# A fused transformer block on one core: where the bias corner is masked, where the DRAM weight sums are issued, and the order of folds and splits in the FFN

## What is computed

```python
def first_block(x, ...):
    h = rms_norm(x, g_pre_mix)
    x = x + rms_norm(chunk_relpos_attention(h, w_qkv, w_o, rel_bias), g_post_mix)
    h = rms_norm(x, g_pre_ffn)
    x = x + rms_norm((silu(h @ w_gate) * (h @ w_up)) @ w_down, g_post_ffn)
    return x
# attention: 16 heads of 64; chunk c of 64 tokens sees the chunks max(0, c-8)..c;
# scores get rel_bias[head, clip(512 + i - j, -63, 128) + 63], then softmax, then @ v
```

## Time and profile before

| | us |
|---|---|
| median of 3 runs | 1453.14 |
| lowest, highest | 1451.38, 1453.32 |
| the profiled execution | 1452.84 |
| its span | 1451.1 |
| PE busy in it | 1293.3 (89%) |
| DVE busy | 806.8 (56%) |
| ACT busy | 624.9 (43%) |
| POOL busy | 83.3 (6%) |

### The profile page before, as it was taken

One profiled execution on the slowest core, in us unless ns is written; L12 is line 12 of the kernel. 1 busy time (PEld: TensorE's weight loads), 2 busy tenths in 40 slices (PEclk: granted clock), 3 DMA queues, 4 the chain that ended last, 5 costly groups with the idle time before them and its releaser, 6 DMA issues.

```text
span 1451.1 us, 18423 instructions
## 1 busy us (share of the span) xinstructions
PE 1293.3 (89%) x7031; PEld 1106.7 (76%) x7031; DVE 806.8 (56%) x1469; ACT 624.9 (43%) x1169; POOL 83.3 (6%) x145
## 2 busy tenths in 40 slices
PE   9998354545998898889999999999999999999998
PEld 7886242433897898888877888888887878898987
DVE  5374222332675554458776656777554553687574
ACT  5374222332544343345554543246433553354543
POOL 1011111111100000000001101000000000000000
PEclk9999676767999999999999999999999999999999
DMA  6479999999743544444653449941222213244542
GB/s 220 138 205 322 269 291 268 272 267 284 205 145 127 193 146 145 151 169 177 213 190 117 146 142 309 308 125 58 87 89 87 87 37 109 88 150 155 174 144 89
DMA packets 41448, 250.32 MB, mean 173 GB/s; under 512 B 5000, under 2 KB 5260, under 8 KB 13840
## 3 DMA queue, kind: packets, MB, share of 16 engines
q1 hardware_dynamic: 26952, 160.07, 31.1%
q0 software_dynamic: 11520, 83.89, 21.9%
q10 hardware_dynamic: 2888, 5.18, 1.0%
HBM read 240.72 MB, written 88.09 MB: 227 GB/s over the span
## 4 chain that ended last, share of the span: by engine, by line
PE 73%; DMA 18%; issue 3%; DVE 3%; ACT 1%; POOL 1%; ACTq 0%; SPq 0%; DVEq 0%; POOLq 0%
PE bank L2158 19%; PE bank L2160 19%; PE bank L2159 19%; DMA sum_dram<-in_weights 10%; DMA sum_dram<-sum_dram 8%; PE sc L2158 2%; PE sc L2160 2%; PE sc L2159 2%; PE sc L2335 1%; PE ob L2359 1%; PE tp L2344 1%; DVE w_lo L1349 1%; PE bank L2276 1%; POOL rstd L652 1%; PE bank L2285 1%
## 5 line engine op out<-in xcount | busy, mean ns | idle before, releaser
L1349 DVE TENSOR_TENSOR w_lo<-w_raw,w_hi 128x512 fp32r<-128x512 f32 (+1 forms) x427 | 331.4, 821 | 217.1 <-ACT w_hi L761 216.3
L2158 PE MATMUL bank<-xT_hi,w_hi 128*128 128x512 f32 (+1 forms) x960 | 360.5, 376 | 22.7 <-issue 22.6
L761 ACT ACTIVATE w_hi<-w_raw 128x512 fp32r<-128x512 f32 (+1 forms) x427 | 287.3, 728 | 172.5 <-PE bank L2160 124.8
L2159 PE MATMUL bank<-xT_lo,w_hi 128*128 128x512 f32 (+1 forms) x960 | 346.6, 361 | 0.0
L2160 PE MATMUL bank<-xT_hi,w_lo 128*128 128x512 f32 (+1 forms) x960 | 346.3, 361 | 0.0
L2158 PEld LDWEIGHTS bank<-xT_hi,w_hi 128*128 128x128 f32 x960 | 189.4, 197 | 50.9 <-issue 28.4
L2160 PEld LDWEIGHTS bank<-xT_hi,w_lo 128*128 128x128 f32 x960 | 188.8, 197 | 26.4
L2159 PEld LDWEIGHTS bank<-xT_lo,w_hi 128*128 128x128 f32 x960 | 189.6, 198 | 22.8 <-issue 1.2
L2335 PE MATMUL sc<-act_lo,act_hi 128*128 128x128 f32 (+3 forms) x96 | 30.8, 378 | 117.5 <-DVE negmax L1476 117.5
L1476 DVE CUSTOM_DVE_ANT_0 arena<-sc,arena 128x128 f32<-128x128 f32 (+1 forms) x64 | 31.2, 488 | 174.8 <-POOL arena L717 155.2
L834 ACT ACTIVATE arena<-arena,negmax 128x128 f32<-128x128 f32 (+1 forms) x96 | 53.5, 557 | 161.5 <-DVE negmax L1476 157.4
(11 more groups left out here) (303 smaller groups left out, 2211.6 us busy)
## 6 DMA issues: line engine op xcount, KB each, us to landing
w_raw<-in_weights SPq DMA_DIRECT2D x94, 1024.0 KB, 4.9
sum_dram<-in_weights POOLq DMA_DIRECT2D x60, 1024.0 KB, 12.1
w_raw<-sum_dram SPq DMA_DIRECT2D x40, 1024.0 KB, 4.8
sum_dram<-sum_dram POOLq DMA_DIRECT2D x20, 1024.0 KB, 15.1
arena<-in_bias ACTq DMA_DIRECT2D x16, 256.0 KB, 8.2
act_lo<-act_lo SPq DMA_DIRECT2D x24, 128.0 KB, 8.2
x_sb<-in_x SPq DMA_DIRECT2D x4, 512.0 KB, 6.7
w_raw<-in_weights SPq DMA_DIRECT2D x4, 512.0 KB, 8.7
```

The source lines that it names most:

```text
L761: nc.scalar.activation(w_hi[SPLIT_AT[b]][:, cols], w_raw[SLOT[b]][:, cols], ACT.Copy)\
L1349: nc.vector.tensor_tensor(w_lo[SPLIT_AT[b]][:, cols], w_raw[SLOT[b]][:, cols], w_hi[SPLIT_AT[b]][:, cols].bitcast(F32), ALU.subtract).then ...
L2158: nc.tensor.matmul(ps, hi_l, hi_r, start=first, stop=False, skip_group_check=onto)
L2159: nc.tensor.matmul(ps, hi_l, lo_r, start=False, stop=False, skip_group_check=onto)
```

## The change

- **Bias corner.** POOL writes the corners of the four bias buffers once, at its start (`corner_masked`). A bias load is now two DMAs, which leave the corner out: the rows 64 to 127 whole, and the rows 0 to 63 without the last 64 columns. DVE waits for both DMAs itself, and for `corner_masked` at the first four heads.
- **Sums.** POOL issues the transfers of the eight FFN groups in one run, right behind the roots of the first norm, with the same steps in the same order, and takes up the roots of "post1" and "pre1" behind them. The sums for the gates stay where they are.
- **FFN order.** In each up quad DVE folds t3 (`up_add(q, 4, ...)`) ahead of the split of block up + 6. In the down stage the first two gains stand at n = 12 (before: 16), and the update of tile 1 at n = 18 (before: 17). Around the start of a_v, the four parts of the split of its second block are placed otherwise between squares, gains and updates, on ACT and DVE.

```diff
+            for place in biases:
+                nc.gpsimd.memset(place[0:CHUNK, BIAS_W - CHUNK:BIAS_W], NEG).then_inc(corner_masked, 1)
...
-            for h in range(HEADS):
-                pool.wait_ge(bias_loaded[h % 4], 16 * (h // 4 + 1))
-
-                nc.gpsimd.memset(biases[h % 4][0:CHUNK, BIAS_W - CHUNK:BIAS_W], NEG).then_inc(bias_ready, 1)
-                add_weights(SUM_STEPS[h])
+            def add_weights(groups):
+                step_between(sums_of_groups(groups[0::2]), 3 * len(groups), sums_of_groups(groups[1::2]))
+
+            add_weights(range(UP_QUADS + N_DOWN))
             reciprocal_roots("post1", "pre1")
...
-                    act.dma_start(biases[h % 4], dram["bias"][h, :, :]).then_inc(bias_loaded[h % 4], 16)
+                    for rows, cols in ((slice(CHUNK, P), slice(0, BIAS_W)), (slice(0, CHUNK), slice(0, BIAS_W - CHUNK))):
+                        act.dma_start(biases[h % 4][rows, cols], dram["bias"][h, rows, cols]).then_inc(bias_loaded[h % 4], 16)
...
-                            dve.wait_ge(bias_ready, h + 1)
+                            dve.wait_ge(bias_loaded[h % 4], 32 * (h // 4 + 1))
+                            if t == 0 and h < 4:
+                                dve.wait_ge(corner_masked, h + 1)
...
+                up_add(q, 4, p5, 2, 2)
                 split(up + 6)
-                up_add(q, 4, p5, 2, 2)
...
-                if n == 16:
+                if n == 12:
                     for t in range(2):
                         gain_down(t, 0, p1[:, t, :], p1[:, t, :], False).then_inc(gained, 1)
+                if n == 16:
                     for t in range(2):
                         gain_down(t, 1, u2[:, t, :], u2[:, t, :], True)
...
                 if n == 17:
                     update(0)
+                if n == 18:
                     update(1)
-                if n == 18:
                     scale("pre2", 0)
...
             gain_c21(2)
             variance("post2", 2, D)
+            step(parts, 2)
+            update(2)
             step(parts, 1)
-            update(2)
             gain_c21(3)
             variance("pre2", 2, D)
+            variance("post2", 3, D)
+            scale_x("pre2", 2)
             step(parts, 1)
-            scale_x("pre2", 2)
-            variance("post2", 3, D)
-            step(parts, 2)
             update(3)
```

More of the change, by code:

```diff
@@ L96 @@
 MHA_AT, MHA_FIRST_AT, PAIR_AT, ONE_AT = (1, 3, 5, 7), (3, 5, 7), (0, 4), (0,)
-SUM_STEPS = [0] * 4 + [2] * 12
 TAIL_AT = (1, 3, 5, 6, 8, 9, 11, 12, 14, 15), (1, 2, 4, 5, 7, 8)
@@ L439, in build @@
         bias_loaded = [sem(f"bias_loaded{i}") for i in range(4)]
-        bias_ready = sem("bias_ready")
+        corner_masked = sem("corner_masked")
         q_rounded, k_rounded, first_split, k_split = sem("q_rounded"), sem("k_rounded"), sem("first_split"), sem("k_split")
@@ L703, in sums_of_weights, with sums_of_groups @@
                 yield
-            def every_second(groups):
+            def sums_of_groups(groups):
                 for g in groups:
                     yield from sums_of_weights(g)
-            weight_sums = [every_second(range(i, len(GROUPS), 2)) for i in range(2)]
-            def add_weights(steps):
-                step_between(weight_sums[0], steps, weight_sums[1])
-            for h in range(HEADS):
-                pool.wait_ge(bias_loaded[h % 4], 16 * (h // 4 + 1))
-                nc.gpsimd.memset(biases[h % 4][0:CHUNK, BIAS_W - CHUNK:BIAS_W], NEG).then_inc(bias_ready, 1)
-                add_weights(SUM_STEPS[h])
+            def add_weights(groups):
+                step_between(sums_of_groups(groups[0::2]), 3 * len(groups), sums_of_groups(groups[1::2]))
+            add_weights(range(UP_QUADS + N_DOWN))
             reciprocal_roots("post1", "pre1")
@@ L736, in _ @@
                                         fill=ACAUSAL, base=0, pattern=[[-1, P]], channel_multiplier=1).then_inc(score_masked, 1)
-            add_weights(6)
+            add_weights(range(UP_QUADS + N_DOWN, len(GROUPS)))
             for i in range(2):
-                pool.wait_ge(chain_summed[i], 16 * 6 * len(GROUPS) // 2)
-                pool.wait_ge(pair_summed[i], 16 * 2 * len(GROUPS) // 2)
+                pool.wait_ge(chain_summed[i], 16 * 3 * len(GROUPS))
+                pool.wait_ge(pair_summed[i], 16 * len(GROUPS))
             reciprocal_roots("final")
@@ L1070, in _ @@
             squares_c21(2)
+            step(parts, 2)
+            squares_x(2, 2)
             step(parts, 1)
-            squares_x(2, 2)
             squares_c21(3)
-            step(parts, 3)
+            step(parts, 1)
             round_xT("pre2", 2)
```

## The result

The changed kernel takes 1366.79 us (median of 4 runs, 1366.2 to 1371.78) against 1453.06 us for the kernel before in the same session: ratio 0.9416, interval 0.9393 to 0.944. That is 86.3 us; 72.6 were forecast. The forecast time was 1380.5 us, so the kernel came out 13.7 us faster than that. The profiled execution took 1367.32 us, its span is 1365.6, 85.5 less than before.

A forecast was written before the change was run, and what follows sets the result against it. The prediction took the weight sums, bound by the DMA engines and ahead of post1's roots on POOL, as the bound; -41.9 + 2.6 - 31.0 - 1.2 - 0.8 = -72.3 us from 1452.84 gave 1380.5 us, range 1365 to 1400.

The forecast's parts named there:

- gaps: Rival: early loads fit into gaps of the sums' chains, POOL free at 309 us, 1354 us in all; chance 0.08.
- Nothing moves: Rival: attention waits for the bias DMAs themselves, or roots behind the sums cost what the memsets did; 1453 us; chance 0.02.
- mixing costs twice: Rival: two DMA queues disturb each other in the first 67 us, POOL free 26.8 us later; 1407 us; chance 0.07.
- The wait for weights in the up stage: Rival: in the up stage weight blocks can't keep up, so half the fold's gain goes; 1396 us; chance 0.07.
- The root term: First root of post1 on POOL moves from 377.74 to 335.8 us: -41.9 us, bounds -68.7 and -15.
- if the engines only share their time: Step for the sums: start 67.3 us earlier, 26.8 us of other loads added back, so POOL is free at 335.8 us.
- 377.74 - 155.2: Step for the attention: without DVE's 155.2 us of memset stalls it would let post1 begin at 222.5 us.
- the starving rival: Rival: attention waits for weight loads beside the sums; slower than before if loads land in 26 us or more; chance 0.03.
- Tail: After the first root of post1, PE comes back at the lower clock: +2.6 us, bounds 0 and 5.
- Up stage: Fold ahead of the split in the up quads removes PE stalls and slow matmuls: -31.0 us, bounds -33.4 and -21.4.
- Down stage: One update of 1.24 us leaves the place ahead of the fold for which PE waited 3.48 us: -1.2 us.
- a_v: Third part of the second block's split comes ahead of the norm's scaling: -0.8 us, bounds -3 and +1.

The follow-up runs named there:

- six and four groups ahead: The changed kernel with only six, or only four, of eight FFN groups issued before the roots of post1 and pre1, the others behind: 1314.62 us and 1316.85 us.
- the corner alone: The changed kernel with POOL pacing the sums by heads as before, the bias corner still masked once: 1417.63 us, ratio 0.9769.

## Why the prediction was right, and where it was off

**The range held the result only just.** 1366.79 us is 1.8 us above the lower end of 1365 and below the forecast's own bounds of 1370 to 1392; the range went that far down for the sake of the rival "gaps", whose root at 309 us did not come. All five terms erred in the same direction, by 8.2, 0.9, 1.9, 0.9 and 1.4 us, which adds up to the 13 us by which the forecast was off. That the result fell inside is in part luck.

**The mechanism held.** What binds is the last transfer in POOL's order, not the stalls by name. "POOL, not the attention, releases post1", the last transfer with the root right behind it, no wait for a memset, share near 1 from 20 us on: all there. "Nothing moves", "mixing costs twice" (root at 363) and "gaps" (root at 309) fall with the root at 327.67. The wait for weights in the up stage didn't come with this change; it came as soon as transfers were left for that stage (six and four groups ahead). So the rival had a real mechanism, with the condition that the DMA engines are full there.

**The root term was mis-sized: -50.1 instead of -41.9.** The step "if the engines only share their time" charged the 26.8 us of early loads in full. The run of sums, from the first issue to the last, took 308.1 us (18.98 to 327.12) against 288.1 before (87.45 to 375.51), so only 20 us were added. The missing 8 us come apart, roughly, so:
- The start was 68.5 us earlier, not 67.3, since the first transfer stood right behind the root and the root itself came 1.1 us earlier: 1.2 us.
- The same bytes took less engine time. Before: 288.9 us at a share of 1.00 plus 68.5 at 0.40 (share sums of the DMA view, 290.0 and 27.4), 317.4 us. After: 308.95 us at 1.02, 315.1 us. That is 2.3 us. The sums' queue has 80.1% of 308.95 us for 65.55 MB, 3.78 us per MB against 3.79; the loads' queue 2.70 for all its 20.51 MB, the price beside the sums (2.67), and no longer 3.05 as in the quiet stretch.
- The rest, about 5 us, is that the engines were filled more densely. The share adds up the times of the packets, so a share over 1 means that packets' times overlap on an engine. It was 1.00 before and 1.02 after, and 317.4 us of packet time takes about 5 us less at the second than at the first.

The prediction used a share of 1.00 as a wall, and it was not quite one. The bound of -68.7 covered it; the value taken stood too near to "no gain". The Trainium skill ("Trainium Kernel Development and Optimization", Key Constraints) says that the queues of SP, ACT and POOL interleave on the same 16 DMA engines and that issuing from several saves only issue time. The price per MB of the sums' queue agrees (3.78 beside 3.79 us). What the early start won, 50 us, it won because the engines had been idle for 0.60 of the first 67 us.

With the corner alone the same work took 322 us of engine time (291.05 us at 1.01 plus 69.8 at 0.40), 7 more than in the changed kernel. (These sums go by shares of two digits, so they hold to 1 or 2 us.) How much of the price depends on the mixture and how much on the execution, the runs don't tell.

**PE's idle time was 85 us, not 110**, since the attention ended at 242 us, not 222.5. The step "377.74 - 155.2" took all of DVE's stalls as delay of the attention. PE waited for DVE for only 117.5 us of them, which is the idle part of the 291 us in the earlier trace rows (291 - 173.46). 377.74 - 117.5 is 260; the other 18 us are mostly the lower clock: from 20 us to the root PE was busy for 240.5 us before and 221.8 now, with about as many matmuls (1102 and 1121). The early sums also delay the attention: it ended at 242 us beside them and at 235 with the corner alone. The error cost nothing, since 85 us of cover were left, but the end of the attention was the number on which the starving rival and the four groups rest. The landing time on which that rival hangs was 13.6 us, against 14.0 beside the sums before: by its own formula a delay of 1.5 us, where it needed 188.

**Tail, +1.7 instead of +2.6:** within its bounds of 0 to 5.

**Up stage, -32.9 instead of -31.0.** Right in its mechanism: no wait but the one of 1.26 us in the last quad, where 1.2 was forecast. The clock was counted as kept in four quads and lost in the last; it was kept in all five, which is the bound of -33.4.

**Down stage, -2.1 instead of -1.2, and a_v, -2.2 instead of -0.8.** The edit before the last product shortened the wait from 3.48 to 2.28 us, as worked out from half of the 2.48. Around a_v PE waited twice before, for 1.59 and 1.53 us; now it waits once, for 2.37, which is 0.7 less and what was forecast, and the matmul behind it takes 0.50 us instead of 0.80. The excess of both terms is in PE's busy time for the same work, which fell by 0.9 us in the down stage (90.17 to 89.31) and by 1.4 behind it (678.59 to 677.14): fewer matmuls at the lower level, which the forecast had left out. Both terms are as small as the differences between executions.

## What to carry to other kernels

A long wait for a small instruction says what stands ahead of it in its engine's order, and removing the wait is worth only what the next thing in that order allows: look for the transfers, and ask when they could start and what must come behind them at all. An engine that issues chained DMAs and also makes small values on the critical path should get only those transfers ahead of the value that are needed before the value's consumers have used up the rest. An engine's full share of time in one stretch is no reason against moving its work into a stretch where it is idle, and PE waits of 4 us in a dense stretch cost half as much again through the clock.

## What the runs showed of the hardware beyond that

The DMA engines' share reached 1.02 to 1.03 over 160 us with three queues busy, and 101.4% for the sums' queue alone from 248 to 327 us, so "1.00" is not the end of what these engines take by this measure. Loads of 1 MB landed in 13.6 us beside the sums, and in 10.5 to 11.5 us in the up stage of the kernels with groups left over, against 5.1 alone. The same wait of PE, 3.48 us at the same place, was followed by matmuls at the lower level in one trace (0.80 us) and at the full one in another (0.50 us); waits of 4.33 us in the up stage had the lower level behind them each time (a first matmul of 0.55 us, and 0.21 from one to the next instead of 0.12), and one of 1.26 us had not (0.36 us, then 0.28). The length of the wait alone does not settle it: one of 2.28 us in the changed kernel had the lower level behind it (0.79 us), and one of 2.37 us some 29 us later had not (0.50).
